# Moving the last mLSTM head's query and key projections from the attention phase into the mLSTM phase

## What is computed

```
u = x @ w_in
m_qk, m_v, m_o, m_gates, a_q, a_k, a_v = split(u)
h_m = mlstm(silu(conv5(m_qk) + conv_b), m_v, sigmoid(m_o), gates)   # 4 heads of 128, forwards and backwards
h_a = window attention with a sink over (a_q, a_k, a_v)             # 8 heads of 64, 2 key/value heads
mix = concat(h_m, h_a) @ w_out
```

## Time and profile before

| | us |
|---|---|
| median of 3 runs | 3833.89 |
| lowest and highest | 3824.36, 3840.50 |
| the profiled execution's own time | 3823.56 |
| its span in the trace | 3821.9 |
| attention phase, first feed matmul to last instruction (from the trace) | 947.9 to 1194.7 |
| mLSTM phase (from the trace) | 1194.9 to 1341.4 |

### The profile page before, as it was taken

One profiled execution on the slowest core, in us unless ns is written; L12 is line 12 of the kernel. 1 busy time (PEld: TensorE's weight loads), 2 busy tenths in 40 slices (PEclk: granted clock), 3 DMA queues, 4 the chain that ended last, 5 costly groups with the idle time before them and its releaser, 6 DMA issues. The chain is left out here.

```text
span 3821.9 us, 54135 instructions
## 1 busy us (share of the span) xinstructions
PE 3611.6 (94%) x20016; PEld 2845.4 (74%) x20016; DVE 2438.2 (64%) x4242; ACT 1684.6 (44%) x3152; POOL 733.8 (19%) x523
## 2 busy tenths in 40 slices
PE   8999999999998798999999989999888888999998
PEld 5787778776766675888887857777667766888886
DVE  3344343666465748877768874666666658877787
ACT  4355222434466415333344374555533325556443
POOL 1000056243002214322210150000043321000013
PEclk9999999998999998999999999999989999999999
DMA  2100168462111112565546422111111106987662
GB/s 91 33 28 28 64 234 289 132 203 90 39 47 59 50 39 100 200 204 200 183 185 223 132 54 62 47 61 50 72 63 49 54 23 209 351 299 256 219 204 93
DMA packets 229578, 479.94 MB, mean 126 GB/s; under 512 B 31664, under 2 KB 45168, under 8 KB 229320
## 3 DMA queue, kind: packets, MB, share of 16 engines
q1 hardware_dynamic: 229320, 476.52, 36.8%
HBM read 348.96 MB, written 129.44 MB: 125 GB/s over the span
## 5 line engine op out<-in xcount | busy, mean ns | idle before, releaser
L1826 PE MATMUL b_ffn_space<-b_ffn_in_hi,b_ffn_wh 128*128 128x512 f32 x1932 | 756.6, 392 | 8.4 <-DVE b_ffn_in_x_low L1301 3.4
L1828 PE MATMUL b_ffn_space<-b_ffn_in_hi,b_ffn_wl 128*128 128x512 f32 x1932 | 753.2, 390 | 0.0
L1826 PEld LDWEIGHTS b_ffn_space<-b_ffn_in_hi,b_ffn_wh 128*128 128x128 f32 x1932 | 363.7, 188 | 92.1 <-issue 11.2
L1827 PE MATMUL b_ffn_space<-b_ffn_in_x_low,b_ffn_wh 128*128 128x512 f32 x1104 | 430.7, 390 | 0.0
L1828 PEld LDWEIGHTS b_ffn_space<-b_ffn_in_hi,b_ffn_wl 128*128 128x128 f32 x1932 | 363.7, 188 | 76.1
L1827 PE MATMUL b_ffn_space<-b_ffn_in_own_low,b_ffn_wh 128*128 128x512 f32 x828 | 322.7, 390 | 0.0
L1827 PEld LDWEIGHTS b_ffn_space<-b_ffn_in_x_low,b_ffn_wh 128*128 128x128 f32 x1104 | 208.0, 188 | 42.9 <-issue 0.2
L1885 ACT ACTIVATE b_ffn_wh<-b_ffn_raw 128x512 fp32r<-128x512 f32 (+1 forms) x188 | 112.7, 611 | 209.1 <-PE b_ffn_space L1828 207.8
L1711 ACT ACTIVATE b_ffn_wh<-b_ffn_raw 128x512 fp32r<-128x512 f32 x224 | 136.0, 623 | 101.9 <-PE b_ffn_space L1828 101.7
L1827 PEld LDWEIGHTS b_ffn_space<-b_ffn_in_own_low,b_ffn_wh 128*128 128x128 f32 x828 | 155.8, 188 | 31.8
L1717 DVE TENSOR_TENSOR b_ffn_wl<-b_ffn_raw,b_ffn_wh 128x512 fp32r<-128x512 f32 x224 | 159.4, 712 | 14.9 <-ACT b_ffn_wh L1711 14.0
(11 more groups left out here) (702 smaller groups left out, 8909.2 us busy)
## 6 DMA issues: line engine op xcount, KB each, us to landing
b_ffn_raw<-w SPq DMA_DIRECT2D x96, 256.0 KB, 4.0
b_ffn_raw<-w_ffn SPq DMA_DIRECT2D x44, 512.0 KB, 4.2
sums_ahead<-sgu_blocks SPq DMA_DIRECT2D x40, 512.0 KB, 6.0
b_ffn_raw<-sums_ahead SPq DMA_DIRECT2D x80, 256.0 KB, 4.0
sgu_blocks<-w SPq DMA_DIRECT2D x24, 512.0 KB, 6.8
b3f_y<-w SPq DMA_DIRECT2D x24, 512.0 KB, 6.1
b_ffn_sums<-b3f_y SPq DMA_DIRECT2D x24, 512.0 KB, 4.7
b_ffn_raw<-b_ffn_sums SPq DMA_DIRECT2D x48, 256.0 KB, 4.6
```

The lines of the kernel that those rows point to most:

```text
L1826: self.nc.tensor.matmul(acc, self.weights.wh[w][:, wk], high[:, k], start=(k == 0), stop=False)
L1827: self.nc.tensor.matmul(acc, self.weights.wh[w][:, wk], low[:, k], start=False, stop=False)
L1828: last = self.nc.tensor.matmul(acc, self.weights.wl[w][:, wk], high[:, k], start=False, stop=(k == self.plan.rows(s) - 1))
```

## The change

- Attention's feed loses two of its eight convolved slices, the query and the key of the last mLSTM head (slices 3 and 7): 14 blocks become 12, of which nine instead of eleven are spread over the units.
- `SPACE` goes from 6.2 to 5.6. The offsets 6.3 and 10.5 inside a unit stay.
- The mLSTM phase's feed gains these two blocks in front of its four gates. They are planned at 0 and 12.6, for 12.6 each; the gates follow at 25.2, 49.0, 72.8 and 96.6, for 23.8 each, with no gap.
- The convolution's row buffers in the mLSTM phase lie over the second half of `num`, which head 1 fills first, so ScalarE waits for all 20 tap instructions before the first copy of head 1. TensorE waits for both SiLUs before it transposes the keys of head 3, and GpSimd before it prepares head 3.
- The weights fetched ahead during attention are those of slice 3 instead of the first gate.

```diff
-        weights = [d["w_mo"][h] for h in range(M_H)]
-        plan = [((h + 0.6) * HEAD, 0.85 * HEAD) for h in range(M_H)]
-        takes = [None] * M_H
+        late = [n for n in range(2 * M_H) if n % M_H == M_H - 1]
+        weights = [d["w_mqk"][n] for n in late] + [d["w_mo"][h] for h in range(M_H)]
+        plan = [(0.45 * HEAD * i, 0.45 * HEAD) for i in range(2)] + [((h * 0.85 + 0.9) * HEAD, 0.85 * HEAD) for h in range(M_H)]
+        takes = [None] * (2 + M_H)
         feed = Feed(ph, "feed", pair, weights, takes, plan, slots=1, ahead=ahead, fetched=True, after=after)
+        conv = Convolution(ph, "conv", feed, lambda n, tap: cols["m_taps"][:, TAPS * n + tap:TAPS * n + tap + 1],
+                           lambda n: cols["m_conv_b"][:, n:n + 1], lambda n: qk[:, n, :], over=PLACES[num.name] + 4 * 2 * DT * (M_DH + 2))
+        for i, n in enumerate(late):
+            takes[i] = conv.keep(i, n)
...
                 for n in range(1, 2 * M_H):
+                    if n == 2 * (M_H - 1):
+                        pool.wait_ge(conv.smoothed, 2)
                     halves.weigh(pool, n)
...
                             if h >= 3 and half == 0:
                                 pe.wait_ge(mixed, 2 * (h - 2))
+                                pe.wait_ge(conv.smoothed, 2)
...
                             se.wait_ge(out_ready[dr], w + 1)
+                            if h == 1 and k == 0 and dr == 0:
+                                se.wait_ge(conv.tapped, 2 * TAPS * len(late))
...
-                weave(feed.high(se), feed.taking(se), keeping_keys(), exponentials(), weighing(), reading(), deviations())
+                weave(feed.high(se), feed.taking(se), conv.smoothing(se), keeping_keys(), exponentials(), weighing(), reading(), deviations())
...
-                weave(feed.low(ve), weights(), states(), finishing())
+                weave(conv.tapping(ve), feed.low(ve), weights(), states(), finishing())
...
-    PRODUCT, SPACE, HEADS = 10.9, 6.2, 4
-    kinds = ["k", "v", "q0", "c", "q1", "c", "c", "q2", "c", "q3", "c", "c", "c", "c"]
+    PRODUCT, SPACE, HEADS = 10.9, 5.6, 4
+    kinds = ["k", "v", "q0", "c", "q1", "c", "q2", "c", "q3", "c", "c", "c"]
+    early = [n for n in range(2 * M_H) if n % M_H < M_H - 1]
```

More of the change, by code:

```diff
@@ L625, with __init__ @@
 class Convolution:
-    def __init__(self, ph, name, feed, taps_of, bias_of, out_of, before=None, slots=2):
+    def __init__(self, ph, name, feed, taps_of, bias_of, out_of, before=None, slots=2, over=None):
         self.nc, self.feed, self.taps_of, self.bias_of, self.out_of, self.before, self.slots = ph.nc, feed, taps_of, bias_of, out_of, before, slots
-        self.rows = [ph.sb(f"{name}_rows{i}", [P, S + 2 * PAD]) for i in range(slots)]
+        if over is None:
+            self.rows = [ph.sb(f"{name}_rows{i}", [P, S + 2 * PAD]) for i in range(slots)]
+        else:
+            self.rows = [ph.nc.alloc_sbuf_tensor_at(f"{ph.name}_{name}_rows{i}", [P, S + 2 * PAD], F32, offset=over + 4 * i * (S + 8))
+                         for i in range(slots)]
         self.padded = ph.sem(f"{name}_padded")
@@ L3283, in mlstm @@
         for h in range(M_H):
-            takes[h] = gate(h)
+            takes[2 + h] = gate(h)
         def chunk_of(k, dr):
@@ L3541, in finishing @@
                                 for i in range(2):
-                                    ve.wait_ge(feed.taken[i], h + 1)
+                                    ve.wait_ge(feed.taken[i], h + 3)
                             nc.vector.scalar_tensor_tensor(out=qk[:, h, c], in0=turned[:], scalar=cols["m_norm_g"][:, h:h + 1],
                                                            in1=og_of(h)[:, c], op0=ALU.mult, op1=ALU.mult).then_inc(mixed, 1)
-                weave(feed.low(ve), weights(), states(), finishing())
+                weave(conv.tapping(ve), feed.low(ve), weights(), states(), finishing())
 def window_attention(nc, d, consts, cols, pair, v, qk, aq, halves, ahead, after):
-    PRODUCT, SPACE, HEADS = 10.9, 6.2, 4
-    kinds = ["k", "v", "q0", "c", "q1", "c", "c", "q2", "c", "q3", "c", "c", "c", "c"]
+    PRODUCT, SPACE, HEADS = 10.9, 5.6, 4
+    kinds = ["k", "v", "q0", "c", "q1", "c", "q2", "c", "q3", "c", "c", "c"]
+    early = [n for n in range(2 * M_H) if n % M_H < M_H - 1]
     begin = 3 * PRODUCT + 1.0
@@ L3589, in window_attention @@
         for i, kind in enumerate(kinds):
-            weights.append(d["w_mqk"][len(convs)] if kind == "c" else d["w_aqkv"][{"k": 4, "v": 5}.get(kind) or int(kind[1])])
+            weights.append(d["w_mqk"][early[len(convs)]] if kind == "c" else d["w_aqkv"][{"k": 4, "v": 5}.get(kind) or int(kind[1])])
             if kind == "c":
@@ L3602, in window_attention @@
             if kind == "c":
-                takes[i] = conv.keep(i, convs.index(i))
+                takes[i] = conv.keep(i, early[convs.index(i)])
             elif kind in "kv":
@@ L4151, in second_block @@
             halves = HalfHeads(nc, ph, consts, dram, gate_cols, qk, block_sum)
-            window_attention(nc, d, consts, cols, pair, v, qk, aq, halves, ahead, halves_of(d["w_mo"][0]))
+            window_attention(nc, d, consts, cols, pair, v, qk, aq, halves, ahead, halves_of(d["w_mqk"][M_H - 1]))
             mlstm(nc, d, consts, cols, dram, pair, qk, v, gate_cols, halves, ahead, halves_of(d["w_out2"][0]))
```

## The result

The changed kernel took 3844.11 us (median of 11 runs, 3836.37 to 3850.39), the kernel before in the same comparison 3829.10 us (11 runs, 3822.55 to 3840.50). The ratio is 1.004, with a 95% interval from 1.003 to 1.0049: 15 us slower, inside the half per cent that the prediction called no change, and beyond its interval to the side that the forecast of -2.3 us did not have. The time lies 1 us above the forecast's own range (3821 to 3843) and inside the range for 8 in 10 (3813 to 3845).

The account below looks back on a forecast made before the run. TensorE was taken to bound the kernel, busy 94% of the span. Attention -21.0 and mLSTM +18.7 gave -2.3 us, 3831 against the median; own range 3821 to 3843, 8 in 10 3813 to 3845.

Parts of the forecast that it names:

- points 1 and 2: mLSTM phase: two moved blocks bring 21.8 us of TensorE work, and 2.8 groups of the last gate add 1.9.
- point 4: mLSTM loop, first head: feed fills nearly all of 3.5 us TensorE idle, -3.1 us (bounds 0 and -3.5).
- Transfers: mLSTM phase: four more pieces of 256 KB through SP, costed at 0; uncovered, some 4 us.
- Three or four more units may now wait some 0.2 to 0.3 us: +0.8: Attention's unit loop: transposes wait slightly more as spare time shrinks by 0.3 us, leaving a saving of 21.0 of 21.8.
- stay after the change: Seam after attention's loop, 9.3 us: the last slice's taps and SiLU stay uncovered, at the same cost.
- point 5: mLSTM loop, gaps between gate blocks: denser feed fills waits and holds the clock, -6 us (bounds 0 and -8).
- Point 3: Start of the mLSTM phase: the first feed group waits for its weights to be rounded, +1.6 us (bounds 0.7 and 3).
- Point 6: mLSTM phase: moved taps and SiLUs crowd VectorE and ScalarE, +2.5 us (lower bound 0).
- The unit's chain becomes attention's bound: Rival, attention: transposes wait in every unit, pitch stays near 6.3 us; total +17 to +20 us; chance 0.06.
- the 5.8 us that was to prove it: Sign in attention's unit loop: a pitch over 5.8 us would show that the chain's rival is right.
- VectorE becomes the bound of the first heads: Rival, mLSTM phase: taps slowed beside GpSimd hold up state updates, total +14 us, 3848; decides past 1.3 us per tap; chance 0.06.

Follow-up runs that it names:

- no_conv: Changed kernel with the two moved slices only projected and copied, their taps and SiLUs left out: 3844.93 us, against the changed kernel's 3844.11.
- gp_small: GpSimd's mLSTM additions and products cut to a sixteenth of their columns, except the first half head: 3809.12 us on the kernel before, 3823.47 on the changed kernel.
- all five rows: Five profiled kernels with the changed mLSTM code, moved taps included (the changed kernel and four variants of attention or spacing): mLSTM phase 172.7 to 178.3 us.

## Why the prediction was wrong

**What held.** TensorE is the bound of attention's loop, and its work there fell by 20.6 us. The two blocks and the 2.8 groups of the last gate were to bring 23.7 us to the mLSTM loop (points 1 and 2); its busy time grew by 23.9. The waits of the first head went, as point 4 had it: from 1189.8 to 1227.8 TensorE isn't idle at all. Transfers cost nothing that shows. Neither VectorE nor ScalarE became the bound of attention, as said: they have 107.0 and 104.0 us in 188.3. The time came 13 us above the 3831 that was said, the change 17 us above -2.3. That the first is smaller is luck: the forecast stood on a median of three runs, 3833.9, and the eleven have 3829.1.

**The step that failed in attention: "Three or four more units may now wait some 0.2 to 0.3 us: +0.8".** The waits in the loop came to 7.7 us of idle more, and the seam to 2.6 us more. The prediction judged the spare time of an average unit, 1.8 us. It didn't lay the smoothings' due times, which follow the feed and not the units, against the new grid of units. A smoothing of 3.7 us is twice the spare time; whether it costs nothing or 2.9 us depends on whether it lies behind both exponentials or between them. The seam was taken to "stay after the change"; in the changed kernel's order the last smoothing but one stands in front of an exponential and a copy of the last units, and TensorE waits 2.58 us (before, 1.71 at the same place):

```profile
1169.81 1.28 ACT L691 ACT_TABLE_LOAD   x1
1171.10 1.15 ACT L691 ACTIVATE b2m_qk<-b2m_qk,all_columns 128x1024 f32<-128x1024 f32 x1
1172.27 1.28 ACT L3771 ACT_TABLE_LOAD   x1
1173.57 0.51 ACT L3771 ACTIVATE gqa_e<-gqa_s,gqa_least 128x257 f32<-128x257 f32 x1
...
1174.60 0.87 PE L3710 MATMUL gqa_o<-gqa_et,gqa_av 128*64 128x128 f32 x10 [2.58 <-ACT gqa_et L3782]
```

The mechanism of the forecast was right and the saving was there to be had: with the smoothings placed and the spacing kept, attention fell by 21.1 us, to 226.0.

**The step that failed in the mLSTM phase: point 5, "I take -6 of some -8".** The first head had 4.2 us of idle and has none, so the later heads went from 14.8 to 17.4; without the moved convolutions (no_conv) the whole loop still has 15.9. Taken by the terms, loop and tail grew by 22.5 us: 23.7 of work, -4.2 for the first head, +4.2 for crowding, which leaves -1.2 for point 5, clock and all (the spread of 5.6 us between profiles of this mLSTM code makes this split rough). Its own bound, "the waits move elsewhere", is what happened. The reading that failed is that of the earlier trace rows: the gaps between gate blocks were only where the waits were seen. The timeline of VectorE in the same microseconds, shown above, has two normalisations in 2.63 us and four in 3.43, beside GpSimd; what made most of the waits were GpSimd's bursts, which hold such instructions back. A denser feed adds to what stands ahead of the probabilities and states: at 1230.52 it is a `low` and two taps, themselves held. Denser feed can hide a held instruction, as in the first head, where a `low` took 1.21 us at 1202.84 and TensorE didn't wait; in the later heads it didn't on balance. gp_small shows the size: the bursts make 12.9 of the 19.0 us of idle before and 11.6 of the 17.4 after.

**Sizes.** Point 3, the start, was put at 1.6 us with a bound of 3. From the first key transpose to the end of the start it is 6.3 us after and 2.6 before, +3.7. Of this 1.93 is a wait for the first `low`, which VectorE began at 1187.6, when ScalarE had rounded the first piece of weights behind its two key copies; and 1.44 is the first feed group itself, at the lower clock of 0.50. Point 6, crowding, was put at 2.5; leaving the moved convolutions out gave back 4.2 of the phase against after, 1 to 6 against all five rows. So of the 18.2 us between -2.3 and +15.9, attention makes 10.7; point 5 4.8, point 3 2.1 and point 6 1.7, less 1.1 that the first head gave beyond its 3.1.

**The rivals.** "The unit's chain becomes attention's bound" did not come: a unit takes 188.3 / 32 = 5.88 us, and the loop's two waits over 1 us, 2.87 and 1.79, lie at single smoothings, not in every unit. The pitch did pass the 5.8 us that was to prove it, so this was a bad test: it tells nothing on whether every unit waits or a few. "VectorE becomes the bound of the first heads" had the right mechanism in the wrong place. It asked whether taps pass 1.3 us on average. They did not: the 16 accumulating taps took 739 to 748 ns each, the four first taps 483 to 1480. The same holding, of normalisations, `low` and first taps, had been making most of the idle time of the kernel before, and that was in the trace: line 3508's longest instruction is 1290 ns beside a median of 280.

## What to carry to other kernels

- Idle time on the bounding engine is room for moved work only if the engine that ends the waits is not the one that the moved work needs as well. Before counting it as free, look what the releasing engine was doing, and whether its instructions take their normal time there: compare the median and the longest of one line.
- A long instruction of a secondary engine (here a SiLU with two table loads, 3.7 us) in a planned order is judged by its place against the spare time of the unit it falls into, not by the engine's load. When a plan's spacing changes, list where each such instruction lands.
- Where GpSimd works beside VectorE on SBUF, the length of one GpSimd instruction counts more than their sum, up to the point at which GpSimd itself comes late: here four pieces made the kernel before 10 us faster by the ratio, and eight made it 7 us slower than it was.

## What the runs showed of the hardware

- A GpSimd addition of 512 columns took 1.05 to 1.33 us by its line's median, of 128 columns 0.40 to 0.46, of 64 columns 0.29 to 0.32, of 32 columns 0.25: a large part does not shrink with the columns.
- Two of VectorE's instructions of 128 columns with all inputs in SBUF (TENSOR_SCALAR and SCALAR_TENSOR_TENSOR of the normalisation) took 280 and 347 ns by the median and up to 1290 and 1361 beside GpSimd; a SCALAR_TENSOR_TENSOR with one input in PSUM stayed at 293 at most, and BATCH_NORM_STATS2, which reads one SBUF tile, at 295. Cutting GpSimd's columns freed 17.9 of VectorE's 85.7 busy us in the loop.
- Behind one wait of 2.87 us, TensorE's granted clock stayed at 1.00 in one profiled run and was 0.72 over the next 6 us in another, with the same waits ahead of it.
